# Shifting one of three interleaved mixers by 2.9 beats against the other two in a two-layer block

## The reference

```
y = rms_norm(x) @ w_in + b_in                  # split by columns
m_out = memory:    mLSTM, 4 heads x 64, with exponential gates over the sequence
h_out = gated:     HGRN2, 4 heads x 64,
        A[l,s] = sum_d q[l,d] * exp(G[l,d] - G[s,d]) * key[s,d]    for s <= l
        o = A @ v
s_out = attention: 8 query heads, 2 key heads, window of 128, one sink a head
x = x + concat(m_out, h_out, s_out) @ w_out
x = x + square(relu(rms_norm(x) @ w_up)) @ w_down
x = x + sigmoid(rms_norm(x) @ w_ple_gate) * rms_norm(p @ w_ple_proj)
```

## Time and profile before

| what | value |
| --- | --- |
| median of three runs | 3261.94 us |
| profiled execution / span | 3265.37 / 3263.6 us |
| PE busy | 3039.0 us, 93% of the span |
| DVE, ACT, POOL busy | 1829.0, 1393.0, 651.6 us |
| mean granted TensorE clock | 0.970 of full speed |
| first mixers stage, first PE work to last attention output | 165.4 to 278.2 us |
| second mixers stage | 906.7 to 1019.5 us |

### The profile page before, as it was taken

How to read it: one execution, slowest core, us unless ns; L and a number is a source line. 1 busy time by engine, 2 the same in 40 slices (tenths; PEclk the granted TensorE clock), 3 DMA queues, 4 the chain that set the end, 5 groups by cost and what they waited for, 6 DMA issues and landing times. The chain is left out here.

```text
span 3263.6 us, 59772 instructions
## 1 busy us (share of the span) xinstructions
PE 3039.0 (93%) x25454; PEld 2413.2 (74%) x25454; DVE 1829.0 (56%) x2665; ACT 1393.0 (43%) x2369; POOL 651.6 (20%) x542
## 2 busy tenths in 40 slices
PE   8989999999978999999989999889689988799999
PEld 6757788887746788887658888767477777588887
DVE  6665543445665543445665736474366766457464
ACT  5555322235455422234464424345365655344242
POOL 1000311212000310212001101143175645011010
PEclk9989999999989999999999999989899999799999
DMA  4101322322101323332012323325311111133232
GB/s 148 52 2 65 104 95 93 97 93 82 59 5 62 95 96 97 95 95 78 1 52 91 110 84 100 103 100 194 133 45 33 42 43 39 47 95 106 84 99 83
DMA packets 82344, 260.72 MB, mean 80 GB/s; under 512 B 9632, under 2 KB 13216, under 8 KB 81824
## 3 DMA queue, kind: packets, MB, share of 16 engines
q1 hardware_dynamic: 71424, 235.39, 22.6%
q10 hardware_dynamic: 10656, 21.50, 1.7%
HBM read 235.89 MB, written 20.97 MB: 79 GB/s over the span
## 5 line engine op out<-in xcount | busy, mean ns | idle before, releaser
L1696 DVE TENSOR_TENSOR mlp_w_lo<-mlp_ring,mlp_w_hi 128x1024 fp32r<-128x1024 f32 (+1 forms) x211 | 251.7, 1193 | 578.5 <-ACT mlp_w_hi L1673 578.4
L1673 ACT ACTIVATE mlp_w_hi<-mlp_ring 128x1024 fp32r<-128x1024 f32 (+1 forms) x211 | 213.2, 1011 | 647.9 <-PE ps L1634 640.9
L1696 DVE TENSOR_TENSOR ffn_w_lo<-ffn_ring,ffn_w_hi 128x1024 fp32r<-128x1024 f32 (+3 forms) x172 | 224.2, 1303 | 440.7 <-ACT ffn_w_hi L1673 440.7
L1673 ACT ACTIVATE ffn_w_hi<-ffn_ring 128x1024 fp32r<-128x1024 f32 (+3 forms) x172 | 187.2, 1089 | 483.3 <-PE ps L1634 477.7
L1633 PE MATMUL ps<-mlp_more_parts,mlp_w_hi 128*128 128x512 f32 x952 | 373.5, 392 | 0.0
L1632 PE MATMUL ps<-tiles_parts,mlp_w_hi 128*128 128x512 f32 x832 | 329.7, 396 | 1.1 <-issue 1.1
L1632 PE MATMUL ps<-ffn_x_parts,ffn_w_hi 128*128 128x512 f32 x792 | 312.4, 394 | 18.1 <-DVE ffn_x_parts L2411 14.2
L1634 PE MATMUL ps<-tiles_parts,mlp_w_lo 128*128 128x512 f32 x832 | 327.7, 394 | 0.0
L1632 PE MATMUL ps<-mlp_more_parts,mlp_w_hi 128*128 128x512 f32 x760 | 306.9, 404 | 21.1 <-DVE mlp_w_lo L1696 12.7
L1633 PE MATMUL ps<-ffn_x_parts,ffn_w_hi 128*128 128x512 f32 x792 | 309.9, 391 | 0.0
L1634 PE MATMUL ps<-ffn_x_parts,ffn_w_lo 128*128 128x512 f32 x792 | 309.8, 391 | 0.0
(11 more groups left out here) (504 smaller groups left out, 6158.0 us busy)
## 6 DMA issues: line engine op xcount, KB each, us to landing
ffn_ring<-in_w_ffn_up SPq DMA_DIRECT2D x88, 512.0 KB, 3.5
mlp_ring<-in_w_up SPq DMA_DIRECT2D x64, 512.0 KB, 3.6
mlp_ring<-in_w_down SPq DMA_DIRECT2D x64, 512.0 KB, 3.6
rwkv_keep<-ffn_ring ACTq DMA_DIRECT2D x64, 256.0 KB, 2.5
sq<-rwkv_keep SPq DMA_DIRECT2D x64, 256.0 KB, 3.1
ffn_ring<-in_w_ffn_down SPq DMA_DIRECT2D x16, 768.0 KB, 4.1
in_ring<-in_w_in SPq DMA_DIRECT2D x22, 512.0 KB, 3.6
mlp_ring<-in_w_in SPq DMA_DIRECT2D x22, 512.0 KB, 3.5
```

The source lines that it names most:

```text
L1673: nc.scalar.activation(w.w_hi[:, n % SPLIT, 0:width], w.ring[:, n % RING, 0:width], ACT.Copy).then_inc(s["w_hi_ready"], 1)
L1696: nc.vector.tensor_tensor(w.w_lo[:, n % SPLIT, 0:width], w.ring[:, n % RING, 0:width], w.w_hi[:, n % SPLIT, 0:width].bitcast(F32), ALU.sub ...
```

## The change

`SCORE` goes from 1 to -1.9: every step of the gated mixer on PE, DVE and ACT gets a beat that is lower by 2.9, relative to the memory and the attention. The mask `never` is made as the second instruction of DVE's list rather than the fourth, and the small product `neg_sink` (L1113) goes from beat 0 to beat 4. No instruction is added or taken away, and none changes its operands.

```diff
 MEMORY, UNIT = 0, 4
 ATTEND, GROUP = 38, 3
-SCORE, LEVEL = 1, 4
+SCORE, LEVEL = -1.9, 4
...
         def attention_dve(dve):
-            yield 0
+            yield MEMORY + UNIT
             nc.vector.tensor_scalar(neg_sink[:], sinks, -1.0, None, ALU.mult).then_inc(s["a_ready"], 1)
...
             yield MEMORY - 5
             nc.vector.tensor_scalar(C_parts[:], m.masks[0:3 * 32, 0:S], 0.0, None, ALU.mult).then_inc(s["c_cleared"], 1)
+            yield MEMORY - 4.5
+            nc.vector.tensor_scalar(never[:], m.masks[:, 0:P], -1.0, -NEG, ALU.add, ALU.mult).then_inc(s["c_parts"], 1)
             yield MEMORY - 4
             dve.wait_ge(s["c_whole"], 1)
             nc.vector.tensor_tensor(C_rest, f.C_rows, C_parts[0:4].bitcast(F32), ALU.subtract).then_inc(s["c_rest"], 1)
             yield MEMORY - 3
             dve.wait_ge(s["c_whole"], 3)
             nc.vector.tensor_tensor(C_parts[64:68], C_rest, C_parts[32:36].bitcast(F32), ALU.subtract).then_inc(s["c_rest"], 1)
-            yield MEMORY - 2
-            nc.vector.tensor_scalar(never[:], m.masks[:, 0:P], -1.0, -NEG, ALU.add, ALU.mult).then_inc(s["c_parts"], 1)
```

## The result

The changed kernel takes 3276.46 us in the median of 22 runs, the kernel before 3264.15 in 22 runs on the same chip. Two of the 22 runs of the changed kernel, slow ones of 4200.70 and 9846.48 us, are left out of the ratio; without them its median is 3275.69. The ratio is 1.0039, with a 95% interval of 1.0030 to 1.0047, so the change costs 10 to 15 us. The forecast was 3267.0 (ratio 1.0016), the range ended at 3275. The time of the third rival, in which the ring starves the clock, is 3274.0 (ratio 1.0037). The forecast stood on 3261.94 for the kernel before; on that base a ratio of 1.0039 is 3274.7, just inside the range, but the change itself was forecast at less than half of its size.

A forecast was written before the change was run, and what follows sets the result against it. PE was busy for 93% of the span, so only idle or half-clock stretches could be won. Stage 1 at +2.4 and stage 2 at +2.7 us made +5.1, a median of 3267.0, range 3257 to 3275.

The forecast's parts named there:

- the ring starves the clock: Rival: idle PE ahead of level 1 and behind level 8 keeps the half clock; +12.1, 3274.0 us, chance 0.20.
- The ring: Levels: each waits for the previous level, S, two exponentials and `decayed`; 39.25 us from S(0) to level 8.
- The clock at the start: +1.2: Idle PE ahead of level 1 delays the full clock, costing 0 to +3.1 us a stage; +1.2 taken.
- PEclk at 0.50 until O(0) has run: Clock staying at 0.50 beyond O(0), early in a stage, would show the forecast to be too fast.
- The waits without a releaser: PE waits between first S and level 8 without visible cause; 0.8 us returns in stage 1, 1.3 in stage 2.
- The start: Up to the first S: the early mask is blocked by POOL's memset, S comes later, +0.8 us a stage.
- Behind level 8: From level 8 to L1486: 17.8 us, midway between full and half clock; -1.5 in stage 1, +0.4 in stage 2.
- The wait ahead of L1327: Gated norm: PE's wait for the reciprocal grows from 3.36 to 3.9 us, +0.5 a stage.
- The mask is not blocked: Rival: the mask goes ahead of POOL's memset at the start, all else as forecast; +2.9, 3264.8 us, chance 0.20.
- the early levels pay: Rival: free mask, no returning waits, clock rising as before, full clock behind level 8; -4.8, 3257.1 us, chance 0.22.

The follow-up runs named there:

- e3: Kernel before with SCORE at -1.9, mask in its old place, level n+1's exponential (ACT) ahead of unit n's and its `decayed` (DVE) ahead of unit n's weighting: ratio 0.9970.
- e5: Kernel before with SCORE at -1.9, mask in its old place, and only ACT's exponential of level n+1 ahead of that of unit n: ratio 1.0043.
- e7: Changed kernel with one unread 128x512 product more on PE, between M(0) and level 1: ratio 1.0023 against the kernel before.
- e8: Changed kernel with 32 unread small products more on PE behind stage 1, shifting later code: ratio 1.0009 against the kernel before.
- e12: Changed kernel with 64 unread small products more on PE behind stage 1, shifting later code: ratio 1.0046 against the kernel before.
- e4: Changed kernel with POOL's three memsets made to wait for the mask: ratio 1.0036 against the kernel before.
- e2: Kernel before with only the mask moved to second on DVE, SCORE as it was: ratio 1.0007.
- e9: Kernel before with 32 unread small products more on PE behind stage 1, shifting later code: ratio 0.9975.
- e10: Changed kernel with POOL's memsets behind the mask, level n+1's exponential and `decayed` moved ahead, 32 small products behind stage 1: 3247.40 us, ratio 0.9951 against the kernel before.
- e11: Kernel before with SCORE at -1.9, mask in its old place, level n+1's exponential and `decayed` moved ahead, 32 small products behind stage 1: 3245.78 us, ratio 0.9955.

## Why the prediction was wrong

**The ring: right.** From the first S to level 1 it forecast 5.65, measured 5.62. Its periods from level 2 on were to be 4.6, 4.4, 5.3, 5.1, 4.6, 4.7; the starts in the rows above are 4.67, 4.35, 5.41, 4.99, 4.90 and 4.53 apart. e3 shows that it is the ring that costs, e5 that its arm over `weighted` grows where the other one shrinks.

**The step that failed: "The clock at the start: +1.2".** The forecast had both ends, 0 and +3.1, and I took the lower part, on the ground that the levels behind are 70 to 95% busy. Level 1 to level 2 took 7.97 instead of 4.9, +3.1, the upper end, by exactly what was named there (level 1, S(1), M(1), O(0) at the half level); e7 gives 3.2 for it by taking it away. In stage 2 it is 6.71, +1.8, which is also the mean of the ten such stages. The busy share of the levels behind, on which the lower part rested, did not bring the clock back early in any of the twelve stages with this hole. With 39.25 for the ring, 3.1 for the clock and no wait for code, stage 1 comes to 42.35; measured 42.44. The rival "the ring starves the clock" named this, and was given 0.20. Its sign, PEclk at 0.50 until O(0) has run, came.

**The second place of the clock was priced nowhere.** I looked at the clock only at the start and behind level 8. It also falls behind level 5, in stage 2 of the changed kernel (level 5 to 6: 9.96 instead of 5.1, of which 2.75 is the wait for code and some 2.1 the clock), in both stages of e8, in stage 2 of e7. The same argument as for the 2.1 ahead of level 1 would have asked for it: the ring has its longest later wait there. And the trace of before had it once, behind the 1.70 of the earlier trace rows and a wait of 1.22; the same product in stage 1 and in stage 2, at the full and at the half clock:

```profile
192.95 1.96 PE L1464 MATMUL ps<-mix_weights,h 128*96 128x512 f32 x4
...
936.57 3.44 PE L1464 MATMUL ps<-mix_weights,h 128*96 128x512 f32 x4
```

**The waits without a releaser: wrongly bounded.** "0.8 and 1.3", up to their whole size of before. Stage 1 has none now, stage 2 has 1.97 and 2.75, 4.7 in all. They are not a stock that comes back in part; they depend on where the list is cut (e8, e12). Stage 2 so is 39.25 + 4.7 + 1.8 + 2.1 = 47.9, measured 48.34. Of the 8.2 us by which the two stages exceed the forecast 5.1, the clock at its two places is 4.6, these waits are 2.6 and the start is 2.1; the rest takes 1.1 back.

**The start: mechanism right, stage 1 too small.** The mask is blocked, 1.90, S 5.36 after the start in stage 2 (+1.0 for 0.8). That the clear ahead of it could be blocked too (2.50), +2.7 for stage 1, I had left out, since it was 0.76 in the earlier trace rows; it isn't so in every run (e7, e8). The trace agrees with the Trainium skill ("SBUF — State Buffer", "Who interferes with whom") in that the other engine blocks fully: by its rule a free mask needs a quiet POOL, and e4's 0.22 shows it. Its effect on the time can't be told from none in e2, nor in e4 against the changed kernel.

**Behind level 8: right in size, on a wrong reading.** -1.9 and +0.6 for -1.5 and +0.4; level 9's first part starts 4.03 behind level 8, as forecast. But the middle between full and half clock was taken because PE would be busy for less than half of the first 6.3 us, "as it was" before. Before, it was busy for 5.30 of them; now it is for 2.93 and 3.85 of 6.18. The wait ahead of L1327 is 3.38 for 3.9, in a stretch of 12.26 for 12.25, and what follows gave the rest back.

**The rivals.** "The mask is not blocked" and "the early levels pay" fell. "The ring starves the clock" is what happened, by its size in the median too, but not place by place: behind level 8, where it had 19.4, the half clock cost only a part (17.39 and 18.02, at a clock of 0.90 and 0.81, with 16.2 for the full clock). It cost behind level 5 in its stead, and 4.7 are waits for code. That its sum comes so near is in part luck.

**Open.** Why the clock rises after 4.7 or 9.8 us of nearly the same work in the two stages of e3, and anywhere between 9.2 and 14.0 with the hole; the traces show that a gap on PE delays it, and that it can be late without one. That the waits without a releaser are waits for the next piece of code is argued from the packets ahead of them and from their moving with the position; no run held a piece back. It is also open whether e4's 5.4 us less in the stages reach the median, which would take more runs.

## What to carry to other kernels

When a step moves between the links of another program, draw the ring of what now waits for what, over all its arms, and look at every place where it leaves TensorE idle: here the idle time was the small part of the cost (3.7 us), the work behind it at the half clock the large one (7.5), and one useless product in the first hole won up to 3.2. Two orders are compared fairly only if the position of their code is: shift both by the same few instructions and see whether the ratio stays. And a stage's time in one profile is one draw: the same list took 110.0 and 114.5 us here, so a term is read over several stages.

## What the hardware showed beyond that

- 32 products of 32x32 that nothing reads, placed behind stage 1, made both kernels faster by 0.25 to 0.30% (e9, and e8 against the changed kernel), 64 of them did not (e12). A wait without a releaser was up to 2.75 us long, and whether stage 2 had one followed the position of its list; in e10 and e11 the 32 left some.
- The wait ahead of level 1 and the clock go together: with none the clock mostly rose 4.0 to 5.9 us after the first S, with 1.11 us after 8.1 and 8.4, with 2.10 us after 9.2 to 14.0. A product of 1.5 us in the hole of 2.10 brought it back to 4.3 and 4.0 (e7).
- The same TENSOR_SCALAR on 96x512 took 0.42, 0.76 or 2.50 us and that on 128x128 0.22, 0.79 or 1.90, by what GpSimd's memsets did beside it. The 0.42 and 0.22 are those of e4 and e10, the only runs without any.
